# The order in which 32 experts' weights are streamed: the place of a rank, from a searched list to the bit reversal

## The reference

```
def moe_ffn(h, w_router, b_router, w_gu, b_gu, w_down, b_down):
    logits = (hf @ w_router).astype(jnp.float32) + b_router.astype(jnp.float32)
    top_val, top_idx = lax.top_k(logits, TOP_K)          # 4 of 32 experts for a token
    gates = jax.nn.softmax(top_val, axis=-1)
    ...
        gu = xb @ w_gu[e] + b_gu[e]                      # 1024 -> 2048
        gt = jnp.minimum(gu[:, :D_FF], SWIGLU_LIMIT)
        up = jnp.clip(gu[:, D_FF:], -SWIGLU_LIMIT, SWIGLU_LIMIT)
        act = (up + 1) * (gt * jax.nn.sigmoid(SWIGLU_ALPHA * gt))
        out = act @ w_down[e] + b_down[e]                # 1024 -> 1024
    ...
    y = jnp.zeros_like(hf).at[row_tok].add(outs.reshape(cap, D_MODEL))
```

## Time and profile before

| | |
|---|---|
| median of three runs | 1440.34 us |
| the profiled execution | 1439.25 us |
| its span | 1437.4 us |
| TensorE busy | 91% of the span |
| VectorE, ScalarE, GpSimd busy | 66%, 43%, 15% |
| moved by DMA | 477.48 MB, 332 GB/s over the span |
| mean granted TensorE clock | 0.96 |

### The profile page before, as it was taken

One profiled execution on the slowest core, in us unless ns is written; L12 is line 12 of the kernel. 1 busy time (PEld: TensorE's weight loads), 2 busy tenths in 40 slices (PEclk: granted clock), 3 DMA queues, 4 the chain that ended last, 5 costly groups with the idle time before them and its releaser, 6 DMA issues.

```text
span 1437.4 us, 25282 instructions
## 1 busy us (share of the span) xinstructions
PE 1312.0 (91%) x6267; PEld 538.2 (37%) x6267; DVE 942.6 (66%) x1594; ACT 624.2 (43%) x682; POOL 221.9 (15%) x152
## 2 busy tenths in 40 slices
PE   4699869699999999999979998899999999999990
PEld 2487448533333333333223332233333333333330
DVE  2999999756666666666546654566666666666665
ACT  3333743434454535353434443353535353535352
POOL 1741244010101010101001100101010101010101
PEclk9899969889999999999999999999999999999996
DMA  9665251789999999599999999998995399999993
GB/s 376 220 233 177 103 195 60 302 327 392 401 400 402 375 410 395 174 395 397 396 405 407 399 409 403 407 403 338 396 402 206 120 403 402 397 400 351 417 373 121
DMA packets 88884, 477.48 MB, mean 332 GB/s; under 512 B 14369, under 2 KB 14881, under 8 KB 38689
## 3 DMA queue, kind: packets, MB, share of 16 engines
q1 hardware_dynamic: 78034, 458.36, 80.1%
q0 software_dynamic: 10832, 18.90, 5.7%
HBM read 464.10 MB, written 20.45 MB: 337 GB/s over the span
## 4 chain that ended last, share of the span: by engine, by line
PE 67%; DVE 9%; SPq 9%; DMA 6%; issue 4%; POOL 2%; ACT 2%; DVEq 0%; ACTq 0%; POOLq 0%
PE ps L1540 37%; PE ps L1552 14%; SPq L320 8%; DMA ring<-in_w_down 4%; PE ps L1532 3%; DMA win<-in_w_in 2%; PE ps L1562 2%; PE ps L1522 2%; PE ps L1333 2%; PE ps L1334 2%; PE ps L1335 2%; DVE ub L1203 1%; DVE ab L1206 1%; DVE ub L1200 1%; DVE catR_lo L1005 1%
## 5 line engine op out<-in xcount | busy, mean ns | idle before, releaser
L1540 PE MATMUL ps<-window,xT 128*64 128x512 f32 x2880 | 641.5, 597 | 6.4 <-ACT window L761 4.8
L1033 DVE COPY window<-ring 128x2048 f32 x360 | 441.9, 1228 | 297.7 <-PE ps L1540 143.3
L1540 PEld LDWEIGHTS ps<-window,xT 128*64 128x64 f32 x2880 | 198.6, 137 | 389.0 <-issue 374.5
L761 ACT ACTIVATE window<-ring 128x2048 f32 x180 | 339.0, 1906 | 7.0 <-DMA ring<-in_w_down 3.1
L1552 PE MATMUL ps<-window,aT 128*64 128x512 f32 x1440 | 336.5, 610 | 3.4 <-DVE window L1033 3.4
L755 ACT ACTIVATE sg<-gb 128x256 f32<-128x256 f32 x90 | 37.5, 416 | 443.2 <-DVE gb L1199 443.2
L561 POOL DMA_INDIRECT y_rows<-osb,idx_c x46 | 75.4, 1639 | 790.0 <-ACT osb L751 772.2
L1552 PEld LDWEIGHTS ps<-window,aT 128*64 128x64 f32 x1440 | 101.4, 140 | 195.1 <-issue 183.8
L1199 DVE TENSOR_SCALAR gb<-ps 128x256 f32<-128x256 f32 x90 | 38.2, 424 | 122.1 <-PE ps L1540 122.1
L751 ACT ACTIVATE osb<-ps,gate_c 128x512 f32<-128x512 f32 x46 | 31.7, 689 | 165.3 <-PE ps L1552 157.8
L548 POOL DMA_INDIRECT xg<-h_rows,idx_n x46 | 45.2, 983 | 263.0 <-DVE idx_n L1079 218.2
(11 more groups left out here) (303 smaller groups left out, 1135.6 us busy)
## 6 DMA issues: line engine op xcount, KB each, us to landing
ring<-in_w_gate_up SPq DMA_DIRECT2D x256, 1024.0 KB, 18.6
ring<-in_w_down SPq DMA_DIRECT2D x128, 1024.0 KB, 17.8
wm<-in_w_mod SPq DMA_DIRECT2D x4, 2048.0 KB, 23.0
wm_a<-in_w_mod SPq DMA_DIRECT2D x4, 2048.0 KB, 8.5
wm_b<-in_w_mod SPq DMA_DIRECT2D x4, 2048.0 KB, 8.7
win<-in_w_in SPq DMA_DIRECT2D x3, 2048.0 KB, 20.1
x_in<-in_x SPq DMA_DIRECT2D x1, 2048.0 KB, 11.9
wo_f<-in_w_out SPq DMA_DIRECT2D x1, 2048.0 KB, 7.4
```

The source lines that it names most:

```text
L761: A(window[c % NW][:, :, :, :], ring_chunk(c, p), ACT.Copy).then_inc(S["moved_b"], 1)
L1033: V.tensor_copy(window[c % NW][:, :, :, :], ring_chunk(c, p)).then_inc(S["moved_a"], 1)
L1540: last = MMUL(ps[M * j:M * (j + 1), h, :].rearrange("m (g n) -> m g n", g=2), xT[:, k, :], window[c % NW][:, k % CK, :, j * GW:(j + 1) * G ...
```

## The change

The list of places is taken out. The place of rank r (0 to 30) becomes the number r + 1 with its five bits read backwards; the last entry stays 0, for expert 0.

```
-PLACE_OF_RANK = (23, 8, 13, 3, 26, 5, 18, 20, 28, 16, 11, 1, 9, 27, 29, 17, 12, 21, 14, 10, 24, 6, 22, 31, 4, 7, 2, 25, 15, 30, 19)
...
-    put("place", np.array([*PLACE_OF_RANK, 0])[None])
+    put("place", np.array([int(f"{r:05b}"[::-1], 2) for r in [*range(1, NE), 0]])[None])
```

## The result

Five timed runs of each kernel: 1438.83 us median before (1434.84 to 1441.77), 1450.81 us after (1448.36 to 1452.19). The ratio of the times is 1.0081, 95% interval 1.0064 to 1.0097: slower by 11.7 us (9.2 to 14.0) of 1440. The forecast was 1453, range 1443 to 1464. The profiled execution after took 1450.81 us, its span is 1449.0 us, 11.6 more than before.

The account below looks back on a forecast made before the run. TensorE and the supply of weights were taken to bound the loop by turns. Between the ledger's +11.7 and the corrected mapped +17.9 it took +14 us, other terms 0: 1439.25 + 14 = 1453.3, given as 1453 us, range 1443 to 1464.

Parts of the forecast that it names:

- Items cost the same, the loop is TensorE's, weights come late in bursts: Loop of 45 items: each still costs 23.85 us of TensorE; 37.8 us excess before, in two groups of late ring loads.
- A supply of 32.6 us per expert: Weight ring: an expert's weights take 32.6 us to arrive, against 23.85 us per block to use.
- a full lead of 18.2 us: Weight ring: a full ring is worth about 18.2 us, lasting two one-block experts; after three the next is 8 us late.
- the ledger: Lead counted place by place, capped by the ring: late weights 37.2 us in old order, 48.9 in new, +11.7 us.
- Late places: Items 11, 17, 22, 35, 40 some 8 to 10 us longer; 21, 39, 44 longer by 1 to 4.
- like in the old order: Second pricing: each late place gets the measured length of its like before; sum 61.7 against 37.9, +23.8 us.
- the rows' 5.9: Three late places after a full ring: fewer rows ahead, at 0.044 us a row, take 5.9 us off the mapped price.
- My +14: Whole kernel: 14 us slower, taken between the ledger's 11.7 and the row-corrected mapped 17.9; bounds 3 and 24 us.
- The row traffic: Gathers and scatters share the DMA engines: 2.5 of the 32.6 us per expert, 18.90 MB coming with rows in use.
- "Faster": Rival, chance 0.07: supply a little quicker in the new order; at 31.0 us per expert 1421, turning point 32.05 us.
- The published limit of about 358 GB/s: HBM transfers: an expert would take at least 35.1 us, orders only 4 us apart; set aside, as the trace disagrees.

Follow-up runs that it names:

- halved loads: Old and new list, each loading only half of every weight chunk from place 2 on: 1403.22 us and 1403.36 us, both 0.9741 of the kernel before.
- the light and the heavy order: New list's blocks by place, one-block experts re-dealt: those in runs of three as light as can be, 1447.95 us, or heavy ones there, 1453.41 us.
- the list with two doubles moved: New list with the two-block experts at places 4 and 20 swapped with the one-block experts at 5 and 21: 1437.05 us, 0.9983 of the kernel before.

## Why the prediction was right

*Items cost the same, the loop is TensorE's, weights come late in bursts.* Right: 23.85 us per item in every kernel, and with halved loads for all 43.

*A supply of 32.6 us per expert, a full lead of 18.2 us.* Right. The steps after have a mean of 32.5, and the ledger places the long items where the trace has them. What it predicted for other lists (place 8 late by only 1.7, where 3.0 was measured, and the signs without rows) was borne out by runs in which only the list or only the traffic differed.

*Late places.* All eight, the last of them hardly (0.8 us). The sizes came out less well than the places: item 40 was 4.3 us long where 8 to 10 were forecast, item 39 6.05 where 1 to 4 were, items 17 and 35 a little under 8. By the two ways of pricing and the measured excess, in us:

| place | ledger | like in the old order | measured |
|---|---|---|---|
| 8 | 8.1 | 10.4 | 9.65 |
| 12 | 8.1 | 10.4 | 7.2 |
| 15, 16 | 2.4 + 8.8 | 3.5 + 10.0 | 3.6 + 8.0 |
| 24 | 8.1 | 10.4 | 7.35 |
| 27, 28 | 2.4 + 8.8 | 3.5 + 10.0 | 6.05 + 4.3 |
| 31 | 2.4 | 3.5 | 0.8 |
| sum | 48.9 | 61.7 | 46.9 |

The pricing by likes was too dear, even with the rows' 5.9 off: 55.8. The 10.4 us of the earlier trace rows came after three singles with 171 rows, the heaviest set that either order has. The ledger was nearer, in part by luck: it has no term for the slow clock. The last 24 matmuls took 7.84, 7.00 and 6.68 us in items 11, 17 and 35 instead of 5.30, so without that the three were 7.1, 5.5 and 6.0 us late, 18.6 in sum, where the ledger has 24.3. The lighter runs, as it seems, and the slow clock partly cancelled. The pair 27 and 28 was 3 us less late in sum than its like, and place 31 hardly late. My +14 lay between the two ways.

*The sum.* The excess grew by 8.3 us in the profiled executions and the span by 11.6. The other 3.3: the first item's matmuls began 2.7 us later, item 44 and the end took 1.0 us more (0.8 of it the late load of place 31) and the first item 0.35 less. So the profile puts 9.1 us down to late weights. With halved loads both lists came to 1403.3 us and reached the loop at the same moment, and so did the kernel before without its rows (item 1 at 320.3 us, 320.5 in the kernel after), so the 2.7 us most likely belong to that one execution of the kernel before, not to the change. The timed ratio says 9.2 to 14.0 us; how much the excess varies from one execution to the next was not measured, and the rest between 9.1 and 11.7 stays open. That the ledger gave 11.7 as well is chance: its two sums are 0.6 under and 2.0 over what the traces show (37.2 for 37.8, 48.9 for 46.9).

*The row traffic.* Right in kind: without it an expert takes 30.0 us and the two lists change places. The size is not settled. Between the light and the heavy order a row cost 0.026 us by the times, which would make the term of 5.9 us 3.5, and 0.016 by the excess; but the three late places for which the term was made, 18.6 us late without the clock, are what the ledger's 24.3 less 5.9 gives. The prediction also let all 18.90 MB come with the rows in use; 2.19 of them stay when the rows are left out.

*The rivals.* "Faster" had its turning point at 32.05 us of supply. At the real supply it did not happen; with the row traffic away, at 30.0, it did, by 11.7 us. The published limit of about 358 GB/s (the Trainium skill, DMA: Bandwidth & Descriptors, Where 436 GB/s comes from) is not what this core met: the late stretches of the kernel after ran at 397 to 412 GB/s, and the one without rows at 420.

## What to carry to other kernels

Where a stream of loads and an engine are nearly in balance on average (here 32.6 us per expert against 45/32 x 23.85 = 33.5), the order of work decides much of what is lost; count the lead as a ledger with the buffer as its cap, and look for the longest run of small work that the buffer survives. Here that run is two, and only from a full ring. A rule that spreads the large experts evenly by place is not the same as one that keeps every run of small ones short, and a margin of 2.6 us in the supply turned the verdict between the same two lists from 12 us slower to 12 us faster.

## What the runs showed of the hardware

The gather and scatter of rows, 16.7 MB in all beside 403 MB of the experts' weights, cost more than their bytes. Without them the late stretch ran at 420 GB/s and an expert took 30.0 us; with them at about 405 GB/s and 32.6 us. By bytes alone (an estimate: 16.7 MB over 2048 rows, 57 rows to a single) it would be 31.1 us. After a wait for weights TensorE's granted clock had means of 0.89 to 0.95 in the long items (items that did not wait show 1.00), and the last 24 matmuls of item 11 took 7.84 us instead of 5.30; in item 40, which was 4.3 us late, the clock stayed at 1.00, while item 11 of the list with two doubles moved, only 3.0 us late, had 0.94.
